# Output projection of a hybrid decoder layer: a second slot for the columns of x, and a hi/lo split without its own buffer

## The chip, the core and the metric

One Trainium2 chip, one of its cores. The metric is the time of one launch in device microseconds (us), the median of the runs shown. A core has TensorE (PE, matrix products; PEld is its loading of weights), VectorE (DVE), ScalarE (ACT), GpSimd (POOL) and SyncE (SP, whose queue issues most DMAs here). The engines run side by side and are ordered by semaphores alone.

## What is computed

One layer step for 1024 prompt tokens and 32 sample tokens (8 sequences of 4), 1056 in all, each of 1024 features, in float32. Cut to what matters here:

```
mixed = concat(rmsnorm(o_attn, g_attn_out), rmsnorm(o_conv, g_conv_out))   # 512 + 512 features
x = x + mixed @ w_o                                                        # output projection, 1024 x 1024
hm = rmsnorm(x, g_mlp_norm)
x = x + square(relu(hm @ w_up)) @ w_down                                   # 1024 -> 4096 -> 1024
gate = sigmoid(rmsnorm(x, g_ple_norm) @ w_ple_gate)
x = x + gate * (p @ w_ple)
```

Ahead of it stand the input norm, the input projection, sliding-window attention and a short gated convolution.

## The kernel before

Everything is held transposed: features on the 128 partitions, tokens along the free axis, in NCH = 3 chunks of 352 tokens. A product of float32 matrices is made from parts: each operand is split into a rounded part (hi) and the remainder (lo), and three products are summed in PSUM: hi x hi, hi x lo, lo x hi (`product`, L1530). A **fill** (L1542) is one output column block of 128 features for one chunk of tokens: 8 input blocks x 3 products = 24 matmuls of 128x128 by 128x352 into one of three PSUM banks, acc[c]. A **unit** is one column block of weights for all three chunks, so three fills. Units are numbered through the kernel; the output projection has 8 (KT), from U_OUT on.

*Weights.* SP loads the unit's 128 columns into w_st (two slots, `load_w` L518); ACT rounds them to w_hi (`split_hi` L799, 1024 elements per partition), VectorE (in the input projection POOL) subtracts to w_lo (`split_lo` L498). The load for a slot waits until the slot's last split is done.

*Output projection, TensorE* (`out_units`, L1717). The residual x lies in DRAM with tokens as rows, so its column block for unit n is loaded into x_col (L263, one buffer of 12 x 128 floats per partition, tokens in groups of 88 rows) and turned by TensorE. For each chunk c: four transpositions of x_col into aux[c] (the semaphore x_turned counts these groups), then the fill into acc[c]. The first group of a unit waits for the unit's weights (wlo_ready) and for the whole column block (xcol_landed):

```
pe.wait_ge(wlo_ready, 2 * i + (U_OUT + s + 1))
pe.wait_ge(xcol_landed, 96 * i + 48 * (s + 1))
```

*SP's queue there* (L578 to L590). A column block takes three DMAs (token_rows, L491: 11 groups of prompt rows, the rest of the prompt, the sample rows), 48 counts of the semaphore. Block 0 is loaded when the last attention tile's scores are done (nm_ready 18). Then, for each unit, in this order on SP's in-order queue:

```
load_w(s, w_o[:, :, bass.ds((2 * i + 2 + s) * P, P)], 2 * i + (U_OUT + 1 + s))
sp.wait_ge(x_turned, 6 * i + 3 * (s + 1))
load_xcol(2 * i + 1 + s)
```

So weights n+2 are loaded, then, when all three groups of unit n are turned, block n+1 into the one buffer. The up-projection's weights (`load_block`, L593) come behind the last block.

*Output projection, ACT* (L1037 to L1048). Per unit, first the split of the next unit's weights; then per chunk: copy of the turned x from aux[c] to xt (L1043), the square of the new xt into sq_new (L1046), and the rounding xg_hi from xg_tmp (L1048).

*Output projection, VectorE* (L1397 to L1414). Per unit the w_lo split of the next unit; then per chunk: xt = acc + xt (L1405), which frees acc[c]; xg_tmp = xt times the gain of the norm (`scale_x` L1385, printed under L1387); sq_sum += sq_new (L1412); xg_lo = xg_tmp - xg_hi (`lo_of_x` L1389, printed under L1392). The scaling's two buffers (xg_tmp) lie behind x_col in memory.

*After it.* Three ones-products (`ones_product` L1736) sum the squares over the features; ACT takes roots and VectorE reciprocals (rstd). The MLP (`mlp_block` L1747) runs 8 blocks of 4 up units and 4 down units; a down unit makes 6 fills of 12 matmuls (2 column blocks x 3 chunks). The **last** block's down units do for the gate's norm what the output projection does for the MLP's: VectorE adds (L1449), scales into xg2_tmp (`scale_x`, also L1387) and, one fill later, subtracts (L1392, `down` L1443); ACT squares (L1097) and rounds (L1099); POOL adds the squares (L793). In each such unit ACT's split of the next weights stands ahead of its squares, VectorE's ahead of its adds. Then 8 gate units (`gate_units`, L1792) with the per-layer embedding, whose results are turned back (`turn_y`) and stored.

*Memory.* place (L172) lays buffers over one another by offset: from p_at on (L262) lie x_col, xg_tmp and root (for the roots), and later p_nat over all of them.

Of the kernel before, what the change touches and what calls it, by code (L numbers as in the profile page):

```python
# [19 lines left out]
F32 = mybir.dt.float32  # L20
# [5 lines left out]
P = 128  # L26
# [113 lines left out]
def hybrid_step(nc, ins, outs):  # L140
# [121 lines left out]
    p_at = cursor[0]  # L262
    x_col = place("x_col", [P, NX, P], F32)  # L263
    xg_tmp = place("xg_tmp", [P, 2, CH], F32)
    root = place("root", [P, 2, CH], F32)

# [7 lines left out]
    rstd = place("rstd", [P, NT], F32)  # L274
    relu_at = cursor[0]
    relu = place("relu", [P, 2, CH], F32)
    relu2 = place("relu2", [P, 2, CH], F32)
    xg2_tmp = place("xg2_tmp", [P, 2, CH], F32, relu_at)
    pw_st = place("pw_st", [P, 2, PLE], F32)
# [10 lines left out]
    with ctx:  # L290
# [25 lines left out]
        vc_landed = sem("vc_landed")  # L316
        xcol_landed = sem("xcol_landed")
        p_landed = sem("p_landed")
# [60 lines left out]
        x_turned = sem("x_turned")  # L379
        xg_scaled = sem("xg_scaled")  # L380
        xg_hi_ready = sem("xg_hi_ready")
# [125 lines left out]
        def _(sp):  # L507
# [69 lines left out]

            def load_xcol(n):  # L578
                for (rows, slots), src in token_rows(x_p, x_s, bass.ds(n * P, P)):
                    sp.dma_start(x_col[rows, slots, :], src).then_inc(xcol_landed, 16)  # L580

            sp.wait_ge(nm_ready, 18)
            load_xcol(0)
            with sp.Fori(0, KT // 2 - 1) as i:
                for s in range(2):
                    load_w(s, w_o[:, :, bass.ds((2 * i + 2 + s) * P, P)], 2 * i + (U_OUT + 1 + s))
                    sp.wait_ge(x_turned, 6 * i + 3 * (s + 1))
                    load_xcol(2 * i + 1 + s)
            sp.wait_ge(x_turned, 3 * (KT - 1))
            load_xcol(KT - 1)  # L590

# [205 lines left out]
        def _(act):  # L798
# [238 lines left out]
            for n in range(KT):  # L1037

                split_hi((n + 1) % 2, 16 * ((U_OUT + n + 1) // 2 + 1), NCH * (U_OUT + n))
                for c in range(NCH):  # L1040
                    f = NCH * n + c
                    act.wait_ge(x_turned, f + 1)
                    act.activation(xt[:, n, chunk(c)], aux[c][:, 0:CH], ACT.Copy).then_inc(aux_free[c], 1)  # L1043
                    act.wait_ge(acc_free[c], U_OUT + n + 1)
                    act.wait_ge(summed, 3 * CT + f)
                    act.activation(sq_new[:, :], xt[:, n, chunk(c)], ACT.Square).then_inc(squared, 1)  # L1046
                    act.wait_ge(xg_scaled, f + 1)
                    act.activation(xg_hi[:, n, chunk(c)], xg_tmp[:, f % 2, :], ACT.Copy).then_inc(xg_hi_ready, 1)  # L1048

# [39 lines left out]
            for m in range(BLK):  # L1089
                down_split(NBLK - 1, m)  # L1090

                for f in range(2 * NCH):
# [3 lines left out]
                    act.wait_ge(summed, 3 * CT + 3 * KT + k)  # L1096
                    act.activation(sq_new[:, :], xt[:, 2 * m + n2, chunk(c)], ACT.Square).then_inc(squared, 1)  # L1097
                    act.wait_ge(xg_scaled, 3 * KT + k + 1)
                    act.activation(xg_hi[:, 2 * m + n2, chunk(c)], xg2_tmp[:, k % 2, :], ACT.Copy)\  # L1099
                        .then_inc(xg_hi_ready, 1)  # L1100

# [41 lines left out]
        def _(dve):  # L1143
# [240 lines left out]

            def scale_x(n, c, tmp, gain):  # L1385

                dve.tensor_scalar(tmp, xt[:, n, chunk(c)], gain, None, ALU.mult).then_inc(xg_scaled, 1)  # L1387

            def lo_of_x(n, c, tmp, k):  # L1389

                dve.wait_ge(xg_hi_ready, k + 1)
                dve.tensor_tensor(xg_lo[:, n, chunk(c)], tmp, xg_hi[:, n, chunk(c)], ALU.subtract)\  # L1392
                    .then_inc(xg_lo_ready, 1)
# [3 lines left out]
            with dve.Fori(0, KT // 2) as i:  # L1397
                for s in range(2):
                    split_lo(dve, 1 - s, 2 * i + (U_OUT + s + 2))
                    n = bass.ds(2 * i + s, 1)  # L1400
                    for c in range(NCH):
# [4 lines left out]
                            .then_inc(acc_free[c], 1)  # L1406
                        dve.wait_ge(acc_free[c], 2 * i + (U_OUT + s + 1))
                        scale_x(n, c, xg_tmp[:, f % 2, None, :], vec[:, bass.ds(2 * i + (V_MLP + s), 1)])

                        dve.wait_ge(squared, 6 * i + (3 * CT + f + 1))  # L1410
                        dve.wait_ge(summed, 6 * i + (3 * CT + f))
                        dve.tensor_tensor(sq_sum[:, chunk(c)], sq_sum[:, chunk(c)], sq_new[:, :], ALU.add)\  # L1412
                            .then_inc(summed, 1)
                        lo_of_x(n, c, xg_tmp[:, f % 2, None, :], 6 * i + f)  # L1414

# [27 lines left out]
            def down(i, m, last, before=None):  # L1443
                split_lo(dve, 1 - m % 2, 8 * i + (U_MLP + BLK + m + 2))
                for f in range(2 * NCH):
# [5 lines left out]
                    if last:  # L1451
                        k = 2 * NCH * m + f
                        dve.wait_ge(acc_free[f % 3], G_BLK * i + (U_MLP + BLK + 2 * m + f // 3 + 1))
                        scale_x(n, c, xg2_tmp[:, k % 2, :], vec[:, V_PLE + n:V_PLE + n + 1])
                        if k:
                            lo_of_x(*before)
                        before = (n, c, xg2_tmp[:, k % 2, :], 3 * KT + k)
                return before if last else None
# [63 lines left out]
        def _(pe):  # L1522
# [194 lines left out]
            def out_units(i, first):  # L1717
                for s in range(2):
                    pe.wait_ge(wlo_ready, 2 * i + (U_OUT + s + 1))
                    pe.wait_ge(xcol_landed, 96 * i + 48 * (s + 1))  # L1720
                    for c in range(NCH):
                        pe.wait_ge(aux_free[c], 2 * i + (OUT_USE[c] + s))
                        turn(aux[c], [((every, slice(k * XT, (k + 1) * XT)), x_col[0:XT, XPC * c + k, :])
                                      for k in range(XPC)]).then_inc(x_turned, 1)
# [150 lines left out]
```

## Time and profile before

| what | us |
|---|---|
| runs, lowest / median / highest | 1411.52 / 1413.66 / 1415.51 |
| span of the profiled execution (first to last instruction) | 1409.7 |
| the profiled execution's own time | not listed apart from the three runs |
| PE busy / weight loads | 1315.8 (93%) / 1298.5 (92%) |
| VectorE busy | 716.3 (51%) |
| ACT busy | 401.9 (29%) |
| POOL busy | 199.2 (14%) |
| mean granted clock of TensorE over the span | 0.980 of full |

The span is one execution on the chip; the runs are timed apart from it. Busy time counts instructions of the engine; matmuls are pipelined, and their ends are modelled, so two that follow each other overlap in the rows. In timelines the number in brackets is the engine's idle time ahead of the instruction and what ended it. Nearly all products stand under L1534 (`product`), all transpositions under L1549 (`turn`), all loads of x_col under L580.

### The profile page before, as it was taken

What the parts mean: (1) busy time and instruction counts of PE and PEld (TensorE: products, weight loads), DVE (VectorE), ACT (ScalarE), POOL (GpSimd) and SP (SyncE); (2) the same over time, 40 slices, a digit from 0 to 9 for tenths busy, and PEclk for the clock granted to TensorE, in tenths of its full rate; (3) what the DMA queues carried; (4) which work ended last, traced back from release to release, by engine and by line L of the source; (5) the groups of instructions that cost most, each with busy time, mean ns of one, the idle gap of its engine ahead of it and who ended that gap; (6) DMA issues with size and microseconds to landing.
All of it is one profiled execution on the core that took longest, in us unless ns stands there. A gap on an engine that the chain in (4) does not pass through costs nothing.

```text
span 1409.7 us, 21751 instructions
## 1 busy us (share of the span) xinstructions
PE 1315.8 (93%) x8348; PEld 1298.5 (92%) x8348; DVE 716.3 (51%) x1271; ACT 401.9 (29%) x801; POOL 199.2 (14%) x216
## 2 busy tenths in 40 slices
PE   3899988997958889999999999999999999999997
PEld 2899877897958889999999999999999999999997
DVE  6302757677575446435445344354453544587342
ACT  5332445455434222102111011121110211254232
POOL 6623434434130000000000000000000000041000
PEclk9999999999989899999999999999999999999999
DMA  5521011001103221321111111111111111111221
GB/s 153 131 60 32 1 48 30 16 16 35 46 17 75 62 65 41 77 52 45 48 47 54 45 45 45 45 45 45 45 45 45 45 50 39 46 45 54 69 68 46
DMA packets 111132, 70.99 MB, mean 50 GB/s; under 512 B 3226, under 2 KB 109622, under 8 KB 111064
## 3 DMA queue, kind: packets, MB, share of 16 engines
q1 hardware_dynamic: 110584, 68.37, 17.7%
q0 software_dynamic: 480, 1.93, 0.5%
q8 instruction: 33, 0.54, 0.2%
q14 instruction: 19, 0.16, 0.0%
q10 hardware_dynamic: 16, 0.00, 0.0%
HBM read 65.69 MB, written 5.54 MB: 51 GB/s over the span
## 4 chain that ended last, share of the span: by engine, by line
PE 77%; DVE 8%; ACT 4%; issue 4%; DMA 3%; POOL 2%; SPq 1%; DVEq 0%; ACTq 0%
PE acc L1534 71%; PE aux L1549 3%; DMA x_col<-in_x_sample 2%; DVE prob L1265 2%; PE aux L1534 1%; POOL act_lo L669 1%; DVE conv L1365 1%; POOL sq_sum L793 1%; DMA w_st<-in_w_in 1%; PE aux L1682 1%; DVE ropea L1218 1%; DVE o_tok L1305 1%; ACT sq_new L1097 1%; DVE pt_lo L1281 1%; ACT w_hi L805 0%
## 5 line engine op out<-in xcount | busy, mean ns | idle before, releaser
L1534 PE MATMUL acc<-xg_hi,w_hi 128*128 128x352 f32 x960 | 312.0, 325 | 0.0
L1534 PE MATMUL acc<-xg_lo,w_hi 128*128 128x352 f32 x960 | 307.8, 321 | 0.0
L1534 PE MATMUL acc<-xg_hi,w_lo 128*128 128x352 f32 x960 | 307.7, 321 | 0.0
L1534 PE MATMUL acc<-a_hi,w_hi 128*128 128x352 f32 x768 | 247.7, 323 | 0.0
L1534 PE MATMUL acc<-a_lo,w_hi 128*128 128x352 f32 x768 | 246.1, 320 | 0.0
L1534 PE MATMUL acc<-a_hi,w_lo 128*128 128x352 f32 x768 | 245.9, 320 | 0.0
L1534 PE MATMUL acc<-act_hi,w_hi 128*128 128x352 f32 x624 | 215.1, 345 | 13.2 <-issue 12.8
L1534 PE MATMUL acc<-act_hi,w_lo 128*128 128x352 f32 x624 | 208.3, 334 | 0.0
L1534 PE MATMUL acc<-act_lo,w_hi 128*128 128x352 f32 x624 | 208.2, 334 | 0.0
L1449 DVE TENSOR_TENSOR xt<-acc,xt 128x352 f32<-128x352 f32 x192 | 100.3, 522 | 179.1 <-PE acc L1534 178.1
L805 ACT ACTIVATE w_hi<-w_st 128x1024 fp32r<-128x1024 f32 x98 | 102.9, 1050 | 280.0 <-PE acc L1534 273.8
L1534 PEld LDWEIGHTS acc<-xg_lo,w_hi 128*128 128x128 f32 x960 | 180.5, 188 | 0.2
L1534 PEld LDWEIGHTS acc<-xg_hi,w_hi 128*128 128x128 f32 x960 | 180.1, 188 | 0.3 <-issue 0.2
L1534 PEld LDWEIGHTS acc<-xg_hi,w_lo 128*128 128x128 f32 x960 | 180.0, 188 | 0.0
L1534 PEld LDWEIGHTS acc<-a_lo,w_hi 128*128 128x128 f32 x768 | 144.3, 188 | 0.0
L1534 PEld LDWEIGHTS acc<-a_hi,w_hi 128*128 128x128 f32 x768 | 144.1, 188 | 0.0
L1534 PEld LDWEIGHTS acc<-a_hi,w_lo 128*128 128x128 f32 x768 | 143.9, 187 | 0.0
L793 POOL TENSOR_TENSOR sq_sum<-sq_sum,sq_new 128x352 f32<-128x352 f32 x24 | 23.2, 966 | 837.8 <-ACT sq_new L1097 837.8
L1534 PEld LDWEIGHTS acc<-act_hi,w_hi 128*128 128x128 f32 x624 | 124.8, 200 | 14.2 <-issue 13.2
L1068 ACT ACTIVATE a_hi<-relu 128x352 fp32r<-128x352 f32 x96 | 47.9, 499 | 292.6 <-DVE relu L1432 292.6
L1432 DVE SCALAR_TENSOR_TENSOR relu<-acc,rstd 128x352 f32<-128x352 f32 x96 | 50.3, 524 | 154.5 <-PE acc L1534 154.5
L1534 PEld LDWEIGHTS acc<-act_lo,w_hi 128*128 128x128 f32 x624 | 124.7, 200 | 0.0
(199 smaller groups left out, 1598.6 us busy)
## 6 DMA issues: line engine op xcount, KB each, us to landing
w_st<-in_w_up SPq DMA_DIRECT2D x32, 512.0 KB, 4.1
w_st<-in_w_down SPq DMA_DIRECT2D x32, 512.0 KB, 3.4
w_st<-in_w_in SPq DMA_DIRECT2D x18, 512.0 KB, 3.9
w_st<-in_w_o SPq DMA_DIRECT2D x8, 512.0 KB, 4.6
w_st<-in_w_ple_gate SPq DMA_DIRECT2D x8, 512.0 KB, 4.3
x_nat<-in_x_prompt SPq DMA_DIRECT2D x11, 352.0 KB
x_col<-in_x_prompt SPq DMA_DIRECT2D x8, 484.0 KB
out<-y_col SPq DMA_DIRECT2D x8, 484.0 KB
```

The source lines that it names most:

```text
L669: pool.tensor_tensor(act_lo[:, 4 * h:4 * h + 4, cols], h_tmp[:, h, :, :], act_hi[:, 4 * h:4 * h + 4, cols], ALU.subtract).then_inc(h_lo, 1)
L793: pool.tensor_tensor(sq_sum[:, chunk(c)], sq_sum[:, chunk(c)], sq_new[:, :], ALU.add)\
L805: act.activation(w_hi[:, s, :], w_st[:, s, :], ACT.Copy).then_inc(whi_ready, 1)
L1068: act.activation(a_hi[:, m, chunk(c)], relu[:, f % 2, :], ACT.Square).then_inc(a_hi_ready, 1)
L1097: act.activation(sq_new[:, :], xt[:, 2 * m + n2, chunk(c)], ACT.Square).then_inc(squared, 1)
L1218: dve.tensor_tensor(heads(ropea, m), qn, cos[:, None, :].broadcast_to([m, NQ + NKV, HD]), ALU.mult).then_inc(cos_ready, 1)
L1265: e = dve.tensor_tensor_reduce(prob[:, h * 2 * P:(h + 1) * 2 * P] .rearrange("p (s k) -> p s k", s=2), bank[:, cols].rearrange("p (s k) -> ...
L1281: frees(dve.tensor_tensor(pt_lo[0:rows_, cols], bank[0:rows_, 0:width], pt_hi[0:rows_, cols], ALU.subtract), step, t, i)
L1432: dve.scalar_tensor_tensor(out=relu[:, f % 2, :], in0=acc[c][:, 0:CH], scalar=0.0, in1=rstd[:, chunk(c)], op0=ALU.max, op1=ALU.mult)\
L1449: dve.tensor_tensor(xt[:, n, chunk(c)], acc[f % 3][:, 0:CH], xt[:, n, chunk(c)], ALU.add)\
L1534: ins_ = pe.matmul(out, w[a][cols], x[b][tile_], start=(k == 0 and p == 0), stop=(k == len(terms) - 1 and p == 2))
L1549: ins_ = pe.transpose(out[dst], src, ident[0:src.shape[0], 0:src.shape[0]])
```

## The change

x_col gets two slots, each with a semaphore of its own; blocks 0 and 1 are loaded at the start, and then block n+2 into unit n's slot, at the place in SP's queue where block n+1 stood. root moves to p_at, under x_col. The scaled copy of x (xg_tmp, and xg2_tmp in the MLP's last block) goes with its semaphore: ACT makes xg_hi from xt with the gain as the scale of its copy, and VectorE makes xg_lo = xt * gain - xg_hi in one operation with three operands. In the projection the addition to sq_sum now stands directly behind the residual add.

```diff
@@ -260,9 +260,8 @@
     xg_lo = place("xg_lo", [P, KT, NT], F32R)
     xt = place("xt", [P, KT, NT], F32)
     p_at = cursor[0]
-    x_col = place("x_col", [P, NX, P], F32)
-    xg_tmp = place("xg_tmp", [P, 2, CH], F32)
-    root = place("root", [P, 2, CH], F32)
+    x_col = place("x_col", [P, 2, NX, P], F32)
+    root = place("root", [P, 2, CH], F32, p_at)
 
     p_nat = place("p_nat", [P, NX, PLE], F32, p_at)
     cursor[0] = act_at
@@ -272,10 +271,8 @@
     pp_hi = place("pp_hi", [P, 2, NT], F32R)
     pp_lo = place("pp_lo", [P, 2, NT], F32R)
     rstd = place("rstd", [P, NT], F32)
-    relu_at = cursor[0]
     relu = place("relu", [P, 2, CH], F32)
     relu2 = place("relu2", [P, 2, CH], F32)
-    xg2_tmp = place("xg2_tmp", [P, 2, CH], F32, relu_at)
     pw_st = place("pw_st", [P, 2, PLE], F32)
     pw_hi = place("pw_hi", [P, 2, PLE], F32R)
     pw_lo = place("pw_lo", [P, 2, PLE], F32R)
@@ -314,7 +311,7 @@
         smask_landed = sem("smask_landed")
         kc_landed = sem("kc_landed")
         vc_landed = sem("vc_landed")
-        xcol_landed = sem("xcol_landed")
+        xcol_landed = [sem(f"xcol_landed{s}") for s in range(2)]
         p_landed = sem("p_landed")
 
         const_set = sem("const_set")
@@ -377,7 +374,6 @@
         mix_lo = sem("mix_lo")
 
         x_turned = sem("x_turned")
-        xg_scaled = sem("xg_scaled")
         xg_hi_ready = sem("xg_hi_ready")
         xg_lo_ready = sem("xg_lo_ready")
         relu2_ready = sem("relu2_ready")
@@ -575,19 +571,18 @@
                     sp.dma_start(v_p, tok[:, QK:QK + KW]).then_inc(kv_stored, 16)
 
 
-            def load_xcol(n):
+            def load_xcol(s, n):
                 for (rows, slots), src in token_rows(x_p, x_s, bass.ds(n * P, P)):
-                    sp.dma_start(x_col[rows, slots, :], src).then_inc(xcol_landed, 16)
+                    sp.dma_start(x_col[rows, s, slots, :], src).then_inc(xcol_landed[s], 16)
 
             sp.wait_ge(nm_ready, 18)
-            load_xcol(0)
+            for s in range(2):
+                load_xcol(s, s)
             with sp.Fori(0, KT // 2 - 1) as i:
                 for s in range(2):
                     load_w(s, w_o[:, :, bass.ds((2 * i + 2 + s) * P, P)], 2 * i + (U_OUT + 1 + s))
                     sp.wait_ge(x_turned, 6 * i + 3 * (s + 1))
-                    load_xcol(2 * i + 1 + s)
-            sp.wait_ge(x_turned, 3 * (KT - 1))
-            load_xcol(KT - 1)
+                    load_xcol(s, 2 * i + 2 + s)
 
 
             def load_block(i):
@@ -1044,8 +1039,8 @@
                     act.wait_ge(acc_free[c], U_OUT + n + 1)
                     act.wait_ge(summed, 3 * CT + f)
                     act.activation(sq_new[:, :], xt[:, n, chunk(c)], ACT.Square).then_inc(squared, 1)
-                    act.wait_ge(xg_scaled, f + 1)
-                    act.activation(xg_hi[:, n, chunk(c)], xg_tmp[:, f % 2, :], ACT.Copy).then_inc(xg_hi_ready, 1)
+                    act.activation(xg_hi[:, n, chunk(c)], xt[:, n, chunk(c)], ACT.Copy,
+                                   scale=vec[:, V_MLP + n:V_MLP + n + 1]).then_inc(xg_hi_ready, 1)
 
             def roots(bank_of, ones_before, inverted_before):
 
@@ -1094,10 +1089,10 @@
                     k = 2 * NCH * m + f
                     act.wait_ge(acc_free[f % 3], G_BLK * (NBLK - 1) + U_MLP + BLK + 2 * m + f // 3 + 1)
                     act.wait_ge(summed, 3 * CT + 3 * KT + k)
-                    act.activation(sq_new[:, :], xt[:, 2 * m + n2, chunk(c)], ACT.Square).then_inc(squared, 1)
-                    act.wait_ge(xg_scaled, 3 * KT + k + 1)
-                    act.activation(xg_hi[:, 2 * m + n2, chunk(c)], xg2_tmp[:, k % 2, :], ACT.Copy)\
-                        .then_inc(xg_hi_ready, 1)
+                    n = 2 * m + n2
+                    act.activation(sq_new[:, :], xt[:, n, chunk(c)], ACT.Square).then_inc(squared, 1)
+                    act.activation(xg_hi[:, n, chunk(c)], xt[:, n, chunk(c)], ACT.Copy,
+                                   scale=vec[:, V_PLE + n:V_PLE + n + 1]).then_inc(xg_hi_ready, 1)
 
             roots(lambda c: N2_AT[c][0], NCH, NCH)
 
@@ -1382,14 +1377,11 @@
             norm_conv(2)
             mix_conv(2)
 
-            def scale_x(n, c, tmp, gain):
-
-                dve.tensor_scalar(tmp, xt[:, n, chunk(c)], gain, None, ALU.mult).then_inc(xg_scaled, 1)
-
-            def lo_of_x(n, c, tmp, k):
+            def lo_of_x(n, c, gain, k):
 
                 dve.wait_ge(xg_hi_ready, k + 1)
-                dve.tensor_tensor(xg_lo[:, n, chunk(c)], tmp, xg_hi[:, n, chunk(c)], ALU.subtract)\
+                dve.scalar_tensor_tensor(out=xg_lo[:, n, chunk(c)], in0=xt[:, n, chunk(c)], scalar=gain,
+                                         in1=xg_hi[:, n, chunk(c)], op0=ALU.mult, op1=ALU.subtract)\
                     .then_inc(xg_lo_ready, 1)
 
 
@@ -1404,14 +1396,12 @@
                         dve.wait_ge(aux_free[c], 2 * i + (OUT_USE[c] + s + 1))
                         dve.tensor_tensor(xt[:, n, chunk(c)], acc[c][:, None, 0:CH], xt[:, n, chunk(c)], ALU.add)\
                             .then_inc(acc_free[c], 1)
-                        dve.wait_ge(acc_free[c], 2 * i + (U_OUT + s + 1))
-                        scale_x(n, c, xg_tmp[:, f % 2, None, :], vec[:, bass.ds(2 * i + (V_MLP + s), 1)])
-
                         dve.wait_ge(squared, 6 * i + (3 * CT + f + 1))
                         dve.wait_ge(summed, 6 * i + (3 * CT + f))
                         dve.tensor_tensor(sq_sum[:, chunk(c)], sq_sum[:, chunk(c)], sq_new[:, :], ALU.add)\
                             .then_inc(summed, 1)
-                        lo_of_x(n, c, xg_tmp[:, f % 2, None, :], 6 * i + f)
+                        dve.wait_ge(acc_free[c], 2 * i + (U_OUT + s + 1))
+                        lo_of_x(n, c, vec[:, bass.ds(2 * i + (V_MLP + s), 1)], 6 * i + f)
 
             def inverse_root(c, bank, use):
                 dve.wait_ge(aux_free[bank], use + 1)
@@ -1451,10 +1441,9 @@
                     if last:
                         k = 2 * NCH * m + f
                         dve.wait_ge(acc_free[f % 3], G_BLK * i + (U_MLP + BLK + 2 * m + f // 3 + 1))
-                        scale_x(n, c, xg2_tmp[:, k % 2, :], vec[:, V_PLE + n:V_PLE + n + 1])
                         if k:
                             lo_of_x(*before)
-                        before = (n, c, xg2_tmp[:, k % 2, :], 3 * KT + k)
+                        before = (n, c, vec[:, V_PLE + n:V_PLE + n + 1], 3 * KT + k)
                 return before if last else None
 
             with dve.Fori(0, NBLK - 1) as i:
@@ -1717,10 +1706,10 @@
             def out_units(i, first):
                 for s in range(2):
                     pe.wait_ge(wlo_ready, 2 * i + (U_OUT + s + 1))
-                    pe.wait_ge(xcol_landed, 96 * i + 48 * (s + 1))
+                    pe.wait_ge(xcol_landed[s], 48 * i + 48)
                     for c in range(NCH):
                         pe.wait_ge(aux_free[c], 2 * i + (OUT_USE[c] + s))
-                        turn(aux[c], [((every, slice(k * XT, (k + 1) * XT)), x_col[0:XT, XPC * c + k, :])
+                        turn(aux[c], [((every, slice(k * XT, (k + 1) * XT)), x_col[0:XT, s, XPC * c + k, :])
                                       for k in range(XPC)]).then_inc(x_turned, 1)
                         pe.wait_ge(att_lo, c + 1)
                         pe.wait_ge(mix_lo, c + 1)
```

## Rows read from the trace of the kernel before

**Rows 1.** The page's chain that ended last, by line, shares of the span.

```profile
PE acc L1534 71%; PE aux L1549 3%; DMA x_col<-in_x_sample 2%; DVE prob L1265 2%; PE aux L1534 1%; POOL act_lo L669 1%; DVE conv L1365 1%; POOL sq_sum L793 1%; DMA w_st<-in_w_in 1%; PE aux L1682 1%; DVE ropea L1218 1%; DVE o_tok L1305 1%; ACT sq_new L1097 1%; DVE pt_lo L1281 1%; ACT w_hi L805 0%
```

**Rows 2.** Stretches: length; PE, PEld, DVE, ACT, POOL busy; PEclk, DMA share, GB/s.

```profile
455.70:472.40 16.70, 14.22 (x84) 13.95 (x84) 7.16 (x13) 4.99 (x10) 0.00 (x0) 0.90 0.29 64
505.80:520.40 14.60, 12.71 (x85) 12.39 (x84) 7.16 (x13) 4.87 (x10) 0.00 (x0) 1.00 0.16 39
...
426.50:537.40 110.90, 96.73 (x590) 94.69 (x589) 50.91 (x93) 35.36 (x72) 0.00 (x0) 0.92 0.27 63
600.00:1100.00 500.00, 500.00 (x3147) 500.00 (x3146) 220.32 (x367) 74.28 (x105) 0.00 (x0) 1.00 0.16 46
```

**Rows 3.** Chain inside the output projection, 426 to 545 us: start, duration, what.

```profile
426.56 0.30 PE aux L1549 x4
426.87 3.85 PE acc L1534 x24
...
469.69 4.95 DMA x_col<-in_x_sample
...
474.76 0.52 PE aux L1549 x4
475.28 5.42 PE acc L1534 x24
...
508.19 3.87 PE acc L1534 x24
...
533.42 3.88 PE acc L1534 x24
```

**Rows 4.** Who waited for whom, 426.5 to 537.4 us: total, times, longest.

```profile
PE aux L1549 <- DMA x_col<-in_x_sample: 14.2, 6, 2.6
...
ACT w_hi L805 <- DMA w_st<-in_w_up: 2.0, 1, 2.0
```

**Rows 5.** SP's queue in order of time, 340 to 545 us: start, duration.

```profile
371.85 0.38 SPq L580 DMA_DIRECT2D x_col<-in_x_sample  x1
383.43 0.42 SPq L522 DMA_DIRECT2D w_st<-in_w_o  x1
...
468.62 0.97 SPq L580 DMA_DIRECT2D x_col<-in_x_prompt  x2
```

**Rows 6.** The page's DMA issues; last number: us from issue to landing.

```profile
w_st<-in_w_o SPq DMA_DIRECT2D x8, 512.0 KB, 4.6
```

**Rows 7.** VectorE in order of time in the output projection.

```profile
505.95 0.53 DVE L1405 TENSOR_TENSOR xt<-acc,xt 128x352 f32 x1 [2.00 <-PE acc L1534]
```

**Rows 8.** VectorE by line: count: min/median/max ns, first and last start.

```profile
L1387 DVE TENSOR_SCALAR xg_tmp<-xt,vec x48: 402/404/907, 423.8 to 1275.6; 128x352 f32 x24, 128x352 f32<-128x352 f32 x24
...
L1392 DVE TENSOR_TENSOR xg_lo<-xg_tmp,xg_hi x48: 510/524/990, 424.9 to 1277.4; 128x352 f32 x24, 128x352 fp32r<-128x352 f32 x24
...
L1320 DVE SCALAR_TENSOR_TENSOR conv<-conv,vec,root_c x12: 572/573/2897, 393.6 to 417.2; 128x352 f32<-128x352 f32 x12
```

**Rows 9.** ACT copies by line, with and without a gain per partition.

```profile
L1007 ACT ACTIVATE conv<-u_p,vec x4: 1149/1150/1151, 151.5 to 377.2; 128x1024 f32<-128x1024 f32 x4
...
L805 ACT ACTIVATE w_hi<-w_st x98: 1039/1046/1102, 12.8 to 1370.9; 128x1024 fp32r<-128x1024 f32 x98
```

**Rows 10.** Groups by form, 1230 to 1278 us: busy, mean ns, idle before.

```profile
L793 POOL TENSOR_TENSOR sq_sum<-sq_sum,sq_new 128x352 f32<-128x352 f32 x24 | 23.2, 966 | 837.8 <-ACT sq_new L1097 837.8
...
L1387 DVE TENSOR_SCALAR xg_tmp<-xt,vec 128x352 f32<-128x352 f32 x24 | 14.5, 606 | 0.9
...
L501 DVE TENSOR_TENSOR w_lo<-w_st,w_hi 128x1024 fp32r<-128x1024 f32 x4 | 4.9, 1226 | 4.1 <-ACT w_hi L805 4.1
```

**Rows 11.** Chain in the last block of the MLP.

```profile
1182.97 57.30 PE acc L1534 x360
```

**Rows 12.** TensorE's waits, 540 to 1410 us.

```profile
PE aux L1549 <- DVE y_ch L1511: 0.9, 1, 0.9
```

**Rows 13.** POOL in order of time, 378 to 422 us.

```profile
392.86 3.24 POOL L752 TENSOR_TENSOR act_lo<-qkv,act_hi 128x1408 fp32r<-128x1408 f32 x1 [1.40 <-ACT act_hi L961]
```

## The prediction, made before the changed kernel was run

> **What bounds the kernel now.** I read the chain that ended last first, then the chain inside the output projection, then who waited for whom, then the clock by stretch. The chain by line [rows 1] is TensorE's products at 71%; one other name in it belongs to this change, the loads of x_col at 2%. So time is won only where TensorE stands still or runs slowly, and the question is where that is. In the long middle of the MLP it does neither: busy 500.00 of 500.00 us at a granted clock of 1.00, the upper of its levels, 2.4 GHz [rows 2].
>
> The output projection is different [rows 3]. Its 8 units each run three times a transposition group (x4) and a fill (x24). Unit 1, which starts at 426.56 us, is clean: a group takes 0.30 to 0.32 us and a fill 3.85 or 3.86, and nothing lies between them, so a unit takes 3 x (0.31 + 3.855) = 12.49 us. The later ones start late: in unit 4 the load of x_col is issued to its last part at 469.69, takes 4.95 us, and only then, at 474.76, the first transposition runs. Six units (2 to 7) wait like this; the list of waits has them as 14.2 us, 6 times, longest 2.6 [rows 4]. The cause is in the order of SP's queue: with one buffer, the load for unit n+1 can't be issued before unit n's third group has read the buffer, which leaves one fill (3.85 us) to cover an issue of 0.97 us for the two long parts plus the third part and 4.95 us of transfer [rows 3, 5]. 1 + 0.1 + 4.95 + 0.1 - 3.85 is about 2.3 us per unit, and 14.2 / 6 = 2.37.
>
> The stall costs a second time. Behind it the group takes 0.52 us instead of 0.31, and the first fill 5.42 instead of 3.86 [rows 3]: the granted clock of such a unit is 0.90, which mixes full clock with a stretch at half, 1.2 GHz [rows 2]. One of the six escapes: unit 6's first fill takes 3.87 us, and its stretch stands at 1.00 [rows 2, 3].
>
> **The change part by part.**
>
> *Two slots of x_col, loads two units ahead.* Units 0 and 1 are both loaded at the start; the load for unit n+2 is issued where that for n+1 was, after unit n's third group. It must then be there when unit n+1 has run its whole 12.49 us besides unit n's last fill: about 16.3 us of cover against some 6.2 us of issue and transfer. The six waits go. Saved: 14.2 us of idle; 5 x (5.42 - 3.86) = 7.8 us of half-clock fills (five of six units); 6 x (0.52 - 0.31) = 1.3 us in the groups. Sum 23.3 us. The same from the ends of the stage: it runs from 426.56 to 533.42 + 3.88 = 537.30, that is 110.74 us, and seven clean units take 7 x 12.49 = 87.4, difference 23.3.
>
> *What is late next.* With the wait gone a unit needs its weights split and its banks free. The weights of unit n+3 are still issued behind an x_col load, at the end of unit n, land in 4.6 us [rows 6], and are needed by ACT only when unit n+1 has ended: 12.5 us against 4.6. VectorE's last add of a unit waits 2.00 us for TensorE, not the other way round [rows 7]. In the stage VectorE is busy 50.91 of 110.90 us and ACT 35.36 [rows 2]; pressed into 87.4 us and less what the change removes they stay at (50.91 - 9.7 + 1.2) / 87.4 = 49% and (35.36 + 2.4) / 87.4 = 43%. Nothing takes the wait's place.
>
> *SP's queue.* The load of unit 1's block moves ahead of the third weight load. SP is idle from 372.2 (the last part of unit 0's load) to 383.43 [rows 5]; another 2.5 us of issue fits there, at no cost. At the end of the stage the first load of up-projection weights is no longer behind the last x_col load; ACT's 2.0 us wait for it [rows 4] goes, but TensorE doesn't wait there: 0.
>
> *hi/lo split in the projection.* 24 scalings on VectorE of 0.404 us go [rows 8]. The subtraction becomes an operation with three operands; the nearest row with that form takes 0.573 where the old subtraction took 0.524 [rows 8], +0.05 each. ACT's copy gets a gain per partition as its scale: the nearest pair of rows is a copy of 128x1024 with such a scale, 1.150 us, and without, 1.046 [rows 9], so +0.10 on each. VectorE now waits for ACT's squares with nothing to do meanwhile; queued behind that wait are the add to sq_sum, the subtraction and the next chunk's add, which has 2.00 us of slack [rows 7]. All of it lies beside TensorE's fills: 0. If that cover were gone, it would be 24 x (0.15 - 0.40) = -6 us on these engines, still a relief.
>
> *The same in the last block of the MLP.* Here VectorE is near TensorE's pace: per fill 0.53 (add) + 0.61 (scaling, held up by the POOL add beside it) + 0.53 (subtraction) + 1.23/6 (weight split) = 1.87 us [rows 7, 8, 10], against 57.30 x 12 / 360 = 1.91 us of TensorE [rows 11]. Without the scaling, and with 0.57 for the subtraction, it is 1.30. Since TensorE doesn't wait in that block, a gain is not possible there; the one wait of TensorE that follows is 0.9 us at the first gate unit [rows 12], so the most that can come back is 0.9. At the other end, ACT's longer copy stands ahead of the next weight split four times, +0.4 us. Both act on the same chain and partly cancel; I take 0, between them, and the ends stay for the range.
>
> A rule of the Trainium skill speaks against this part. The rows show a VectorE operation that takes longer beside POOL's adds: the scaling's mean is 0.606 us in this block against a median of 0.404 over all [rows 8, 10]. "SBUF — State Buffer", section "Who interferes with whom", says that a VectorE instruction with two inputs in SBUF and a GpSimd instruction that reads SBUF exclude each other, the later one waiting for all of the earlier. By the rows I take nothing for it; by the rule the subtraction could wait for the whole of POOL's add each time, which is the third rival below.
>
> **The sum** is against one profiled execution, whose span is 1409.7 us. Its time outside the span is not listed; the median of the runs, 1413.66, is 3.96 us above the span, and I leave that as it is. Span 1409.7 - 23.3 = 1386.4; median 1413.66 - 23.3 = **1390.4**, 1.6% less.
>
> **The rivals.**
> 1. *The idle goes, the half clock stays* (the slow fills come from the pattern of this stage and not from the wait). For it: unit 6 waits too and stays at full clock, so wait and clock are not one to one. Against: clean units of the same stage and the whole MLP hold 1.00 [rows 2, 3]. Then 14.2 + 1.3 = 15.5 us are saved: 1398.2.
> 2. *The load was not the last to come*: something else that is due at a unit's start holds TensorE as long. For it: the list shows only the last of several waits. Against: VectorE and ACT are behind with nothing at a unit's end [rows 7], and the weights are split a unit earlier. Time: no change, 1413.7.
> 3. *The last block becomes bound by VectorE*, since the subtraction now takes the holding-up that the scaling took. Per fill at worst 0.57 + POOL's whole 0.97 [rows 10] + 0.53 + 0.20 = 2.27 against 1.91; 24 x 0.36 = 8.6 us, 1399.0. For it: the scaling's 0.606. Against: the longest old subtraction, with two inputs in SBUF as well, is 0.990 [rows 8], and at that length the sum is 1.72, below 1.91. "SBUF — State Buffer" would give this case; so far the rows bear it out for single operations and not for the loop.
> 4. *Slower*: one mechanism, the same holding-up at its worst row. A three-operand operation took 2.897 us [rows 8] beside a POOL operation of 3.24 us [rows 13]. If each of the 24 new subtractions of the last block took that, VectorE would need 0.53 + 2.90 + 0.20 = 3.63 us per fill, 24 x 1.72 = 41 us more: 1390.4 + 41 = 1431.7. It decides from a mean of 2.15 us per subtraction, where 24 x (0.73 + 2.15 - 1.91) eats the 23.3. Against: POOL's operation in that block takes 0.97, not 3.24.
>
> **How the numbers follow.** Forecast 0.84; rival 1 0.05; rival 2 0.03; rival 3 0.06; rival 4 0.02. The range starts at 1390.4 less 0.9 (gate) and 2.1 (the spread of the three runs below their median): 1387.4. The forecast's own upper end is 1390.4 + 0.4 + 1.6 (one half-clock fill where the stage ends) + 2.1 = 1394.5; taking in rival 1 and most of rival 3 it goes to 1398.2. A measurement of this kernel can tell about 0.3% from no change, 4.2 us. Faster by more: forecast, rivals 1 and 3, 0.95; within it: rival 2, 0.03; slower: rival 4, 0.02.
>
> **What the changed profile would show.** Right: no wait of the transpositions on x_col; the seven units from 1 on in 87 to 88 us, each first fill near 3.86; clock 1.00 throughout the stage; x_col loads issued a unit ahead; ACT's copy near 0.60, the subtraction near 0.57 us in the projection; the MLP's products as dense as before. Wrong: a wait of similar length at unit starts under another name (rival 2), first fills of 5.4 us without idle (rival 1), or gaps between fills in the last block, with subtractions over 1.2 us (rivals 3 and 4).

## The result, and the profile after

The changed kernel takes 1391.0 us (the median of 4 runs, 1389.95 to 1392.14) against 1414.59 (4 runs, 1411.52 to 1416.82): ratio 0.9836, 95% interval 0.9817 to 0.9856, that is 23.6 us less, where 23.3 was forecast. The profiled execution has a span of 1390.3 us and took 1392.14. In the runs listed with their spans the time is 1.8 us above the span, in one of them 2.1. The interval alone would allow any saving from 20 to 26 us; that it lies so near the forecast is shown by the stage below, not by the medians.

The page of the changed kernel, the chain that ended last by line, answers to [rows 1]:

```profile
PE acc L1523 76%; PE aux L1538 4%; DVE prob L1260 2%; PE aux L1523 2%; POOL act_lo L664 1%; PE aux L1671 1%; DMA w_st<-in_w_in 1%; DVE conv L1360 1%; DVE ropea L1213 1%; DVE o_tok L1300 1%; DVE ropea L1217 0%; DVE ropeb L1207 0%; DVE pt_lo L1276 0%; PE aux L1622 0%; DVE o_tok L1292 0%
```

The products (L1534 before, L1523 now, since lines moved up) have gone from 71% to 76%, and the loads of x_col are no longer named. The chain inside the projection, 396 to 560 us (start, duration, what), answers to [rows 3]:

```profile
424.89 5.62 PE acc L1523 x24
430.52 0.30 PE aux L1538 x4
430.82 3.85 PE acc L1523 x24
...
443.00 0.30 PE aux L1538 x4
443.30 3.85 PE acc L1523 x24
...
455.48 0.30 PE aux L1538 x4
455.78 3.85 PE acc L1523 x24
...
514.02 3.88 PE acc L1523 x24
```

Units 1, 2 and 3 start at 430.52, 443.00 and 455.48: one in 12.48 us. From the first group of unit 1 to the end of the last fill it is 514.02 + 3.88 - 430.52 = 87.38 us, where before had 110.74: 23.36 us less. Behind the stage nothing moved: from the end of that last fill to the end of the span it is 1409.7 - 537.30 = 872.40 before and 1390.3 - 517.90 = 872.40 after.

Busy times and clock of the stage (length; PE, PEld, DVE, ACT, POOL busy; PEclk, DMA share, GB/s), beside [rows 2], and TensorE's line of the waits from 426 to 520 us, beside [rows 4]:

```profile
430.50:518.00 87.50, 87.50 (x590) 87.02 (x588) 43.83 (x72) 35.22 (x72) 0.00 (x0) 1.00 0.32 73
```

```profile
PE aux L1729 <- DVE sq_sum L1401: 0.7, 1, 0.7
```

TensorE is busy for all of the 87.50 us at clock 1.00 (before 96.73 of 110.90 at 0.92), and what it waits for there is the sum behind the last unit, which before has as well. SP's queue, beside [rows 5]:

```profile
375.91 0.37 SPq L576 DMA_DIRECT2D x_col<-in_x_sample  x1
376.32 2.71 SPq L576 DMA_DIRECT2D x_col<-in_x_prompt  x2
379.08 0.37 SPq L576 DMA_DIRECT2D x_col<-in_x_sample  x1
387.41 0.42 SPq L518 DMA_DIRECT2D w_st<-in_w_o  x1
...
439.17 1.00 SPq L576 DMA_DIRECT2D x_col<-in_x_prompt  x2
```

Unit 1's block is issued by 379.45, in the idle time ahead of the third weight load. The load at 439.17 is that of unit 3, which starts at 455.48: 16.3 us of cover, the prediction's number.

**Why the spans differ by 19.4 us and the runs by 23.6.** Unit 1 starts at 430.52, 3.96 us later than in before's profile [rows 3]; of what stands ahead of it, the change moves only the load of unit 1's block, issued from 376.32 on, long after the stretch where part of the time went. Unit 0's load, the one just ahead of it on SP's queue, already has its last part at 375.91 where before has it at 371.85 [rows 5], so 4.06 us later. The stretch from 120 to 180 us and the chain inside it, before and then after:

```profile
120.00:180.00 60.00, 56.87 (x366) 54.58 (x366) 39.77 (x80) 23.59 (x61) 29.07 (x28) 0.97 0.04 10
...
163.41 2.33 PE aux L1682 x18
```

```profile
120.00:180.00 60.00, 56.67 (x336) 54.34 (x335) 36.41 (x77) 20.25 (x48) 26.89 (x25) 0.89 0.04 10
...
164.58 4.20 PE aux L1671 x18
```

The same 18 products took 2.33 us in one execution and 4.20 in the other; the granted clock of the stretch is 0.97 and 0.89. Unit 1's start goes with that clock over the profiles, the experiments below among them: 1.00 and 423.82 (the third); 0.97 and 426.56 (before); 0.91 and 428.14 to 429.25 (the second, fourth, fifth and sixth); 0.89 and 430.35 to 430.55 (after, the first and the seventh). The last two experiments change unit 0 and are left out of this. The second and the fifth load x_col at the old time and the sixth is the changed kernel once more, so the lateness is not the change's. In the medians it is not there: of the 23.6 us the stage accounts for 23.36. Before's profile (1409.7 and 1.8 make 1411.5, the lowest of its four runs) was an early one, and that of after is the longest of its four. Why the clock differs there from one execution to the next stays open.

### The profile page after: what moved, and what is told of

Read it like the earlier page. It is cut to its first block, busy times and chain, and to the rows that moved or that the text cites. A ratio compares the mean times of both kernels' runs of the same rounds, so it can differ in the third digit from the quotient of the medians.

```text
span 1390.3 us, 21716 instructions
## 1 busy us (share of the span) xinstructions
PE 1312.9 (94%) x8348; PEld 1297.4 (93%) x8348; DVE 701.2 (50%) x1223; ACT 403.9 (29%) x801; POOL 198.0 (14%) x216
## 3 DMA queue, kind: packets, MB, share of 16 engines
q0 software_dynamic: 480, 1.93, 0.6%
## 4 chain that ended last, share of the span: by engine, by line
PE 84%; DVE 8%; issue 3%; ACT 3%; POOL 1%; DMA 1%; SPq 0%; DVEq 0%; ACTq 0%
PE acc L1523 76%; PE aux L1538 4%; DVE prob L1260 2%; PE aux L1523 2%; POOL act_lo L664 1%; PE aux L1671 1%; DMA w_st<-in_w_in 1%; DVE conv L1360 1%; DVE ropea L1213 1%; DVE o_tok L1300 1%; DVE ropea L1217 0%; DVE ropeb L1207 0%; DVE pt_lo L1276 0%; PE aux L1622 0%; DVE o_tok L1292 0%
## 5 line engine op out<-in xcount | busy, mean ns | idle before, releaser
L1523 PE MATMUL acc<-xg_hi,w_hi 128*128 128x352 f32 x960 | 312.0, 325 | 0.0
L1523 PE MATMUL acc<-xg_hi,w_lo 128*128 128x352 f32 x960 | 307.8, 321 | 0.0
L1523 PE MATMUL acc<-xg_lo,w_hi 128*128 128x352 f32 x960 | 307.8, 321 | 0.0
L1523 PE MATMUL acc<-a_hi,w_hi 128*128 128x352 f32 x768 | 247.7, 323 | 0.0
L1523 PE MATMUL acc<-a_lo,w_hi 128*128 128x352 f32 x768 | 246.1, 321 | 0.0
L1523 PE MATMUL acc<-a_hi,w_lo 128*128 128x352 f32 x768 | 245.9, 320 | 0.0
L1523 PE MATMUL acc<-act_hi,w_hi 128*128 128x352 f32 x624 | 212.5, 341 | 11.7 <-issue 11.3
L1523 PE MATMUL acc<-act_lo,w_hi 128*128 128x352 f32 x624 | 205.7, 330 | 0.0
L1523 PE MATMUL acc<-act_hi,w_lo 128*128 128x352 f32 x624 | 205.3, 329 | 0.0
L1523 PEld LDWEIGHTS acc<-xg_lo,w_hi 128*128 128x128 f32 x960 | 180.5, 188 | 0.2
L1523 PEld LDWEIGHTS acc<-xg_hi,w_hi 128*128 128x128 f32 x960 | 180.1, 188 | 0.2
L1523 PEld LDWEIGHTS acc<-xg_hi,w_lo 128*128 128x128 f32 x960 | 180.0, 187 | 0.0
L1523 PEld LDWEIGHTS acc<-a_lo,w_hi 128*128 128x128 f32 x768 | 144.3, 188 | 0.0
L1523 PEld LDWEIGHTS acc<-a_hi,w_hi 128*128 128x128 f32 x768 | 144.1, 188 | 0.0
L1523 PEld LDWEIGHTS acc<-a_hi,w_lo 128*128 128x128 f32 x768 | 143.9, 187 | 0.0
L1523 PEld LDWEIGHTS acc<-act_hi,w_hi 128*128 128x128 f32 x624 | 122.5, 196 | 12.8 <-issue 11.7
L1523 PEld LDWEIGHTS acc<-act_lo,w_hi 128*128 128x128 f32 x624 | 122.4, 196 | 0.0
```

The costliest lines, as they stand in the source:

```text
L1523: ins_ = pe.matmul(out, w[a][cols], x[b][tile_], start=(k == 0 and p == 0), stop=(k == len(terms) - 1 and p == 2))
```

## The experiments

Three theories were to be told apart: the gain comes from the time at which the loads are issued (mine); it comes from having two buffers as such; or the new split, with fewer operations on VectorE, carries part of it. And of the clock: half clock follows TensorE's standing still, or belongs to the stage. All ratios are to runs of the kernel before, on the same chip.

**Loads without the split.** Two slots and loads two units ahead, with the old three-step split:

```diff
+    x_col = place("x_col", [P, 2, NX, P], F32)
...
+            for s in range(2):
+                load_xcol(s, s)
...
-                    load_xcol(2 * i + 1 + s)
+                    load_xcol(s, 2 * i + 2 + s)
...
-                    act.activation(xg_hi[:, n, chunk(c)], xg_tmp[:, f % 2, :], ACT.Copy).then_inc(xg_hi_ready, 1)
+                    act.activation(xg_hi[:, n, chunk(c)], xg_lo[:, n, chunk(c)].bitcast(F32), ACT.Copy).then_inc(xg_hi_ready, 1)
```

> Two slots of x_col and loads two units ahead, with the old three-step split (scale on VectorE, round on ACT, subtract on VectorE); the scaled copy goes into xg_lo's own place, since its buffer no longer fits beside the second slot. Theory (all of the gain is the earlier load): 23 us less than before, about 1391; the seven units from 1 on in 87.4 us, no wait on x_col, clock 1.00 there. Rival (the split carries part of the gain): between 1392 and 1414, with waits of TensorE left in the stage or in the last MLP block.

1391.2 us against 1413.98, ratio 0.9831 (0.9813 to 0.985). The list of TensorE's waits has no x_col. From unit 1's first group to the start of VectorE's last add the stage takes 87.58 us; by these marks, which the experiments below use too, the changed kernel has 87.51 and before 110.87. This part alone gives the whole gain: 22.8 us of the medians, and the changed kernel is at 1391.0.

**The split without the loads.** One buffer, loads as before:

```diff
-                    act.wait_ge(xg_scaled, f + 1)
-                    act.activation(xg_hi[:, n, chunk(c)], xg_tmp[:, f % 2, :], ACT.Copy).then_inc(xg_hi_ready, 1)
+                    act.activation(xg_hi[:, n, chunk(c)], xt[:, n, chunk(c)], ACT.Copy,
+                                   scale=vec[:, V_MLP + n:V_MLP + n + 1]).then_inc(xg_hi_ready, 1)
...
-                dve.tensor_tensor(xg_lo[:, n, chunk(c)], tmp, xg_hi[:, n, chunk(c)], ALU.subtract)\
+                dve.scalar_tensor_tensor(out=xg_lo[:, n, chunk(c)], in0=xt[:, n, chunk(c)], scalar=gain,
+                                         in1=xg_hi[:, n, chunk(c)], op0=ALU.mult, op1=ALU.subtract)\
```

> The new split alone, with one slot of x_col and loads as before. Theory: no change, 1414 within 2 us; six waits on x_col of 14 us in all and first fills of 5.4 us as before; ACT's rounding near 0.57 us, the subtraction near 0.58. Rival (the split carries part of the gain): 1 to 20 us less. Rival (VectorE becomes the bound in the last MLP block): up to 8.6 us more.

1412.32 us against 1413.98, ratio 0.9988 (0.9973 to 1.0002): no difference that can be told from none. TensorE's waits in the projection:

```profile
PE aux L1539 <- DMA x_col<-in_x_sample: 14.0, 6, 2.6
```

The row is [rows 4] again (14.2, 6, 2.6). VectorE's relief lies beside the fills, as costed.

**Work in the place of the wait.** The kernel before, with 13 products into a bank that nothing reads, ahead of the wait for x_col in units 2 to 7; their results are not used:

```diff
                     pe.wait_ge(wlo_ready, 2 * i + (U_OUT + s + 1))
+                    if not first:
+                        pe.wait_ge(aux_free[NAUX - 1], aux_uses[NAUX - 1])
+                        for _ in range(13):
+                            pe.matmul(aux[NAUX - 1][:, 0:CH], w_hi[:, s, 0:P], act_hi[:, 0, 0:CH], start=True, stop=True)
                     pe.wait_ge(xcol_landed, 96 * i + 48 * (s + 1))
```

> The kernel before, with 13 products of 128x128 by 128x352 into an unused PSUM bank ahead of the wait on x_col in units 2 to 7 (13 x 0.159 = 2.07 us); their result is used by nothing. Theory (the half clock comes from TensorE standing still): the wait shrinks to 0.3 us a unit at the same unit start, clock 1.00 in the stage, and the 7.8 us of slow fills with the 1.3 us of slow groups come back: 1414.6 - 9.1 + about 0.3 = 1406. Rival (the half clock comes from the pattern of the stage): clock stays at 0.90, 1414.

1406.0 us against 1413.98, ratio 0.9944 (0.9924 to 0.9963). TensorE's wait for x_col, the chain of unit 4 and the clock of that unit:

```profile
PE aux L1549 <- DMA x_col<-in_x_sample: 1.6, 4, 0.6
```

```profile
451.61 2.08 PE aux L1723 x13
453.69 0.05 issue
453.74 0.52 PE aux L1549 x4
454.26 3.88 PE acc L1534 x24
...
453.70:468.70 15.00, 14.80 (x97) 14.47 (x97) 7.32 (x14) 5.15 (x11) 0.00 (x0) 1.00 0.33 72
```

The unit still starts late, now behind 2.08 us of work that serves nothing instead of a wait, and its first fill takes 3.88 us at clock 1.00, where it took 5.42 at 0.90 [rows 2, 3]. All six first fills of units 2 to 7 take 3.85 to 3.91 us here. The stage takes 103.22 us against 110.87: 7.65 less, which is the half clock's share of the 23.3 by itself. So the slow fill follows the standing still. The group keeps its 0.52 also where clock and fill are at their best, so its 0.2 us more are not the clock's, and the 1.3 us that the expectation counted for the groups did not come back. TensorE's products and weight loads around a unit's first group, in the changed kernel (unit 3) and then here (unit 4):

```profile
455.15 0.32 PE L1523 MATMUL acc<-act_hi,w_lo 128*128 128x352 f32 x1
455.16 0.45 PEld L1538 LDWEIGHTS aux<-ident,x_col 88*128 88x128 f32 x4
455.31 0.47 PE L1538 MATMUL aux<-ident,x_col 88*128 88x88 f32 x4
...
453.74 0.35 PEld L1549 LDWEIGHTS aux<-ident,x_col 88*128 88x128 f32 x4 [0.34 <-issue]
453.74 0.52 PE L1549 MATMUL aux<-ident,x_col 88*128 88x88 f32 x4
```

x_col is loaded as the weights of the transpositions. Without a wait this load starts at 455.16 and the group at 455.31, both beside the last product ahead, which ends at 455.47; behind a wait the two start together when the data is there, with nothing running. That overlap of some 0.17 us and a group longer by 0.05 make up the 0.22; no run tests this by itself.

**One buffer, loaded in thirds.** The old buffer and the old split, but the block is loaded in three parts, each as soon as its chunk has been turned:

```diff
+                    for c in range(NCH):
+                        sp.wait_ge(x_turned, 6 * i + 3 * s + c + 1)
+                        load_xcol(c, 2 * i + 1 + s)
...
-                    pe.wait_ge(xcol_landed, 96 * i + 48 * (s + 1))
                     for c in range(NCH):
+                        landed = 16 if c < NCH - 1 else 48
+                        pe.wait_ge(xcol_landed[c], 2 * landed * i + landed * (s + 1))
```

> One slot of x_col and the old split, but the column block is loaded in three parts, one per chunk, each as soon as the chunk's group of the unit before is turned (five DMAs a unit in place of three, three semaphores). Theory (the time of issue counts, not the second slot): every part has 12.5 us of cover, no wait, 87.4 us for the seven units, about 1391. Rival (a second slot is needed, since SP's queue or the smaller transfers come late): waits on x_col remain, over 1395.

1390.7 us against 1413.98, ratio 0.9828 (0.9809 to 0.9847); no wait for x_col, stage 87.56 us. TensorE's only wait from 426 to 545 us:

```profile
PE aux L1751 <- DVE sq_sum L1422: 0.7, 1, 0.7
```

So the second slot is not needed for the gain: what counts is that each part of a load is issued long enough before its use.

**Two slots and the new split, loads at the old time.**

```diff
-            for s in range(2):
-                load_xcol(s, s)
+            load_xcol(0, 0)
...
-                    load_xcol(s, 2 * i + 2 + s)
+                    load_xcol(1 - s, 2 * i + 1 + s)
+            sp.wait_ge(x_turned, 3 * (KT - 1))
+            load_xcol(1, KT - 1)
```

> The changed kernel with its two slots and new split, but the load for unit n+1 issued where the kernel before issued it (behind unit n's third group). Theory (only the time of issue counts): the six waits are back, 14 us in all, with five or six first fills of 5.4 us; 1414 within 2 us. Rival (a second slot helps by itself, or the split does): under 1410.

1415.93 us against 1414.59, ratio 1.0014 (0.9998 to 1.0029), and the wait is back:

```profile
PE aux L1539 <- DMA x_col<-in_x_sample: 14.2, 6, 2.7
```

All of the change but the time of issue, and all of the gain is gone.

**The changed kernel once more,** beside the last and the next:

> The changed kernel once more, for the spread between executions and beside the next kernel. The stage from unit 1's first group to its end takes 87.4 us again, and the rest behind it 872.4; what differs between executions lies ahead of the stage, in how often TensorE falls to half clock in the attention part: span between 1386 and 1391.

1390.96 us, ratio 0.9833 (0.9803 to 0.9863), stage 87.57 us; unit 1 starts at 429.25.

**A smaller lead.** The changed kernel with each load issued behind the next unit's second group:

```diff
-                    sp.wait_ge(x_turned, 6 * i + 3 * (s + 1))
+                    sp.wait_ge(x_turned, 6 * i + 3 * (s + 1) + 2)
```

> The changed kernel, with the load for unit n+2 issued not behind unit n's last group but behind the second group of unit n+1, which leaves two fills and a group, 8.0 us, as cover. Theory (a load needs 1.0 + 0.1 + 5.0 + 0.1 = 6.2 us, and any cover above that is enough): no wait on x_col, 87.4 us for the seven units, 1391. Rival (the load needs more when it runs beside the weights, or the weights behind it come late): waits in the stage, over 1393.

1391.36 us against 1415.63, ratio 0.9823 (0.9796 to 0.9849); SP's queue, then the chain:

```profile
434.85 0.97 SPq L576 DMA_DIRECT2D x_col<-in_x_prompt  x2
...
442.83 0.30 PE aux L1538 x4
443.14 3.85 PE acc L1523 x24
```

Unit 2's load goes out at 434.85, 8.0 us ahead of unit 2's first group at 442.83, and nothing in the stage waits (87.52 us). Some 2 us above the 6.2 that issue and transfer take are enough here; the change's 16.3 buy no more.

**Beyond the change: unit 0.** Its three fills run slowly, each behind a wait for the convolution half of its input (5.62 us for the last one in the chain of after above). In the changed kernel, unit 0's fills now start with the four blocks of the attention half and wait for the other half only then:

```diff
+                        if first and s == 0:
+                            pe.wait_ge(acc_free[c], U_OUT)
+                            for k in range(KT):
+                                if k == KT // 2:
+                                    pe.wait_ge(mix_lo, c + 1)
...
```

> The changed kernel, and in unit 0 of the projection each fill starts with the four input blocks of the attention half as soon as they are split, and waits for the convolution half only then. After the last wait half a fill is left in place of a whole one: 1.9 us less at full clock, up to 2.8 at half; 1388 to 1389.5, so 0.998 of the changed kernel. Rival: the chain of roots and splits on ACT and VectorE paces unit 0, and the time that is won is waited for there: 1391.

1389.15 us, ratio 0.9823 (0.9795 to 0.985), beside 1390.96 for the changed kernel in the same comparison: 1.8 us less in the medians, with intervals that overlap, so not settled by the times. The chain ahead of unit 1:

```profile
422.81 1.64 DVE act_lo L1323
424.45 0.04 issue
424.49 3.74 PE acc L1721 x12
428.23 0.30 PE aux L1538 x4
```

Only 12 products stand behind the wait now, but they run at half clock: 3.74 us, where 12 take 1.93 in the fills of 3.85. Counted from the arrival of its last input, unit 0 ends 1.87 us earlier (5.61 us in the sixth experiment, from 423.64 to 429.25; 3.74 here), as expected; the input itself came 0.85 us later in this execution.

So the same with 12 unread products between the halves of the second and third chunk, as in the third experiment:

```diff
                                 if k == KT // 2:
+                                    if c:
+                                        pe.wait_ge(aux_free[NAUX - 1], aux_uses[NAUX - 1])
+                                        for _ in range(12):
+                                            pe.matmul(aux[NAUX - 1][:, 0:CH], w_hi[:, s, 0:P], act_hi[:, 0, 0:CH],
+                                                      start=True, stop=True)
                                     pe.wait_ge(mix_lo, c + 1)
```

> The kernel with the attention half first, and in unit 0, chunks 1 and 2, 12 products into an unused bank (1.9 us, result unused) between the two halves of the fill, where TensorE waits 1.8 and 2.7 us. If standing still causes the half clock, the last half fill, which took 3.7 us, takes 1.9 to 2.3: 1.4 to 1.8 us less than without, about 1387.5. Rival (the half clock is of another cause): 1389.

1388.24 us against 1415.63, ratio 0.9801 (0.9776 to 0.9826): the lowest median of all kernels here, though its interval overlaps that of the changed kernel, and the kernel of the experiment above was timed beside other runs of before (1414.59). The wait ahead of unit 1 and the chain to it:

```profile
PE aux L1538 <- DVE w_lo L497: 1.6, 1, 1.6
```

```profile
419.79 5.67 DMA out<-tail_tok
...
425.60 1.07 ACT w_hi L800
...
426.69 1.23 DVE w_lo L497
427.93 0.04 issue
427.97 0.52 PE aux L1538 x4
428.50 0.01 issue
428.50 4.05 PE acc L1523 x24
```

The half fills do run at full clock: in the last one the products begin at 424.17 and follow each other every 0.16 us, some 1.9 us for the 12, where above it was 3.74. But unit 1 starts at 427.97 instead of 428.23, and its input came 0.32 us earlier in this execution: from those products' start to unit 1 it is 3.80 us, where it was 3.74. So nothing is gained in these two profiles, since a new wait has taken the place. The weights of unit 1 are split late, because ACT first waits until an output has been stored (419.79, 5.67 us). In the experiment above ACT waited for that store too, but there the slow half fill covered it. Here the expected gain turned into a wait on another chain; that this store could move out of ACT's way wasn't tried.

## Why the prediction was right, point by point

- **The idle and its cause**: right. Where the load is issued earlier, the 14.2 us go (first and fourth experiment); with all else changed and the old time of issue they stay (fifth).
- **The half clock, 7.8 us**: right in mechanism and size. 7.65 us came back by filling the wait alone, so rival 1 falls. What spoke for it, a wait without a slow fill, is real: of the 18 waits in before, the second and the fifth experiment three are followed by a fill of 3.85 to 3.87 us (1.88, 1.93 and 2.20 us), and the other fifteen, among them one of 1.85 and one of 2.19, by fills of 4.98 to 5.43. The length of the wait alone does not tell them apart, and what does stays open.
- **The groups, 1.3 us**: right in size; each takes 0.30 now. It is not the clock, since 0.52 stayed at full clock (third experiment).
- **Nothing late next**: right. VectorE's add still waits for TensorE, 1.77 and 1.91 us where it was 2.00 [rows 7]. VectorE in order of time, from one chunk's add to the next one's:

```profile
501.38 0.52 DVE L1397 TENSOR_TENSOR xt<-acc,xt 128x352 f32 x1 [1.77 <-PE acc L1523]
502.47 0.53 DVE L1401 TENSOR_TENSOR sq_sum<-sq_sum,sq_new 128x352 f32<-128x352 f32 x1 [0.56 <-ACT sq_new L1041]
503.05 0.58 DVE L1383 SCALAR_TENSOR_TENSOR xg_lo<-xt,vec,xg_hi  x1
505.54 0.52 DVE L1397 TENSOR_TENSOR xt<-acc,xt 128x352 f32 x1 [1.91 <-PE acc L1523]
```

  The foreseen wait for ACT's squares is there too, 0.56 us, well inside that slack. VectorE is busy 43.83 / 87.5 = 50% of the stage (49% was worked out) and ACT 35.22 / 87.5 = 40% (43%): its 22 copies take 12.6 us in place of 11.0, but they overlap their neighbours in the rows, and busy time counts an overlap once. Rival 2 falls.
- **The split's operations**: the subtraction takes 0.585 where 0.57 was taken, and ACT's copy with a gain 0.575 against 0.499 without (+0.08, not +0.10). The second experiment confirms the price of nothing, within its interval of -3.8 to +0.3 us.
- **The last block of the MLP**: rival 3's mechanism is there, its price is not. By form, 1210 to 1260 us (busy, mean ns):

```profile
L788 POOL TENSOR_TENSOR sq_sum<-sq_sum,sq_new 128x352 f32<-128x352 f32 x24 | 22.7, 945 | 814.8 <-ACT sq_new L1093 814.8
L1383 DVE SCALAR_TENSOR_TENSOR xg_lo<-xt,vec,xg_hi 128x352 fp32r<-128x352 f32 x24 | 18.3, 763 | 5.4 <-ACT xg_hi L1094 4.9
...
L1439 DVE TENSOR_TENSOR xt<-acc,xt 128x352 f32<-128x352 f32 x24 | 12.4, 518 | 2.8 <-PE acc L1523 2.8
```

  The scaling's holding-up has moved to the subtraction: 0.763 in the mean instead of the 0.57 that I took. Per fill that is 0.52 + 0.76 + 0.20 = 1.48 us of VectorE against TensorE's 1.91, so it binds nothing, and rival 4, which needs 2.15 us per subtraction, is far off. TensorE is busy for the whole of that stretch, at clock 1.00:

```profile
1210.00:1260.00 50.00, 50.00 (x313) 49.58 (x312) 36.62 (x55) 28.67 (x55) 22.68 (x24) 1.00 0.15 46
```

  For one pair in order of time, POOL and then VectorE:

```profile
1227.29 0.95 POOL L788 TENSOR_TENSOR sq_sum<-sq_sum,sq_new 128x352 f32<-128x352 f32 x1 [0.67 <-ACT sq_new L1093]
...
1227.79 0.82 DVE L1383 SCALAR_TENSOR_TENSOR xg_lo<-xt,vec,xg_hi 128x352 fp32r<-128x352 f32 x1 [0.36 <-ACT xg_hi L1094]
```

  The two run beside each other for 0.45 us (1227.79 to 1228.24), and the subtraction is 0.24 longer than alone. The Trainium skill's "SBUF — State Buffer", "Who interferes with whom", has it wait for the whole of the earlier operation, which would give 0.45 + 0.585 = 1.03; the row shows 0.82, and the longest of the 24 takes 0.89, so the direction agrees and the size doesn't, as far as POOL's rough spans let one say.

**Two steps failed,** though the sum held. "The median of the runs, 1413.66, is 3.96 us above the span, and I leave that as it is" treated 3.96 as time that lies around the span. That is 1.8; the other 2.2 was the profiled execution's place below the median. It cost nothing, since difference and not level was carried over, but the "changed span" of 1386.4 came out as 1390.3, which looks like a miss of 3.9 and is the spread ahead of the stage. And the 0.9 us "at the first gate unit [rows 12]" was put in the wrong place: it is TensorE's wait for the last y_ch at the very end of the kernel, in both traces. At the first gate unit only a weight load waited, 0.4 us before and 0.2 after. The range's lower end had no right to those 0.9.

## What to carry to other kernels

When a load waits for its buffer, compare the time from its issue to its first use with issue plus transfer: here 3.85 us stood against some 6.2, and any way of issuing it earlier (another slot, or the same slot in parts) gave the whole gain, while the slot alone gave none. Price a wait of TensorE together with the fill behind it: 14.2 us of idle brought 7.8 us of half clock with them. Compare a stage between two profiles from its own first row to its last, and take the change in total time from medians of runs, since the spans carry what happened ahead of the stage.

## What the runs showed that was not expected

The part of the kernel ahead of the projection varies by some 7 us from one execution to the next (unit 1 from 423.82 to 430.55) with the clock of a few dense stretches, 18 products taking 2.33 or 4.20 us. And keeping TensorE at full clock in unit 0 made its last half fill 1.8 us shorter without bringing unit 1 any closer to the arrival of unit 0's input, because a store of 5.67 us held ACT. The same transposition group took 0.2 us more behind a wait than without one, at full clock as well.
